# A decoder layer on one core: the input's norm ahead of the memory's, and the memory's projections spread over the attention

## The reference

```python
h = rmsnorm(x, norm1_g); z = h @ w_in      # pool 512 | q 1024 | k 128 | v 128 | memory q 512 | gates 3072
y_pool = pool_mixer(u_pool)                # 4 groups, trailing windows 2, 4, 8, 16, then a 128x128 map
y_swa = sliding_attention(rope(q), rope(k), v, sinks)   # 16 heads of 64, 2 key heads, window 128
km, vm = split(rmsnorm(mem, mem_norm_g) @ w_mem_kv)     # 256 tokens x (512 | 512)
y_mem = softmax(qm @ km.T * 128 ** -0.5) @ vm           # 4 heads of 128
x = x + (g0 * (y_pool @ wp) + g1 * (y_swa @ ws) + g2 * (y_mem @ wm)) @ w_out
x = x + peer(rmsnorm(x, norm2_g))          # 128 x 128 single-neuron experts, product keys
return rmsnorm(x, final_norm_g)
```

## Time and profile before

| | us |
|---|---|
| median of 3 runs (lowest, highest) | 2134.08 (2133.06, 2134.82) |
| the profiled execution | 2133.81 |
| its span, first to last instruction | 2132.0 |
| PE busy in the span | 2071.6 |
| VectorE busy | 1226.4 |
| ScalarE busy | 792.1 |
| GpSimd busy | 849.2 |

### The profile page before, as it was taken

One profiled execution on the slowest core, in us unless ns is written; L12 is line 12 of the kernel. 1 busy time (PEld: TensorE's weight loads), 2 busy tenths in 40 slices (PEclk: granted clock), 3 DMA queues, 4 the chain that ended last, 5 costly groups with the idle time before them and its releaser, 6 DMA issues.

```text
span 2132.0 us, 30302 instructions
## 1 busy us (share of the span) xinstructions
PE 2071.6 (97%) x10616; PEld 1708.8 (80%) x10616; DVE 1226.4 (58%) x1851; ACT 792.1 (37%) x1136; POOL 849.2 (40%) x361
## 2 busy tenths in 40 slices
PE   6988899999999999999999999999999999999998
PEld 5766788887888888888888888888888888888886
DVE  6678321112129999777777777025555555555556
ACT  5566522323223222344554455332222222222223
POOL 4411144443335444433333333444444444444443
PEclk9999999999999999999999999999999999999999
DMA  5211022222224444446556556665555555565552
GB/s 207 89 40 40 30 99 96 92 97 89 78 79 133 148 138 147 143 118 191 189 196 197 188 191 197 212 222 219 179 182 196 217 184 179 183 224 189 184 182 102
DMA packets 108516, 323.47 MB, mean 152 GB/s; under 512 B 11200, under 2 KB 11200, under 8 KB 106304
## 3 DMA queue, kind: packets, MB, share of 16 engines
q1 hardware_dynamic: 108192, 322.49, 44.9%
q10 hardware_dynamic: 288, 0.54, 0.1%
HBM read 253.78 MB, written 69.21 MB: 151 GB/s over the span
## 4 chain that ended last, share of the span: by engine, by line
issue 47%; PE 32%; POOL 19%; DMA 1%; POOLq 0%; DVE 0%; SPq 0%; ACT 0%
PE bank L637 32%; POOL w_lo L417 19%; DMA a_in<-a_rows 0%; POOLq L416 0%; DVE x_sb L1384 0%; DMA a_rows<-abuf 0%; POOLq L420 0%; DVE x_sb L1379 0%; DVE wf L1358 0%; POOL mask L401 0%; POOL mask L403 0%; SPq L266 0%; DVE wT_lo L1362 0%; ACT wT_hi L994 0%; POOL mask L398 0%
## 5 line engine op out<-in xcount | busy, mean ns | idle before, releaser
L417 POOL TENSOR_TENSOR w_lo<-raw,w_hi 128x1024 fp32r<-128x1024 f32 x346 | 845.5, 2444 | 1264.1 <-ACT w_hi L763 1264.1
L763 ACT ACTIVATE w_hi<-raw 128x1024 fp32r<-128x1024 f32 x346 | 366.7, 1060 | 1216.5 <-PE bank L440 698.7
L440 PE MATMUL bank<-hT_hi,w_hi 128*128 128x512 f32 x1488 | 590.9, 397 | 0.5 <-POOL w_lo L417 0.4
L440 PE MATMUL bank<-hT_hi,w_lo 128*128 128x512 f32 x1488 | 580.5, 390 | 0.0
L440 PE MATMUL bank<-hT_lo,w_hi 128*128 128x512 f32 x1488 | 579.3, 389 | 0.0
L1362 DVE TENSOR_TENSOR wT_lo<-wf,wT_hi 128x512 fp32r<-128x512 f32 x128 | 313.5, 2449 | 131.0 <-ACT wT_hi L994 131.0
L440 PEld LDWEIGHTS bank<-hT_hi,w_lo 128*128 128x128 f32 x1488 | 279.4, 188 | 59.9
L440 PEld LDWEIGHTS bank<-hT_hi,w_hi 128*128 128x128 f32 x1488 | 279.8, 188 | 58.7 <-issue 3.9
L440 PEld LDWEIGHTS bank<-hT_lo,w_hi 128*128 128x128 f32 x1488 | 280.1, 188 | 56.1 <-issue 0.7
L637 PE MATMUL bank<-w_hi,wT_hi 128*128 128x512 f32 x1024 | 315.3, 389 | 0.1
L637 PE MATMUL bank<-w_lo,wT_hi 128*128 128x512 f32 x1024 | 315.3, 389 | 0.0
(11 more groups left out here) (217 smaller groups left out, 1518.9 us busy)
## 6 DMA issues: line engine op xcount, KB each, us to landing
raw<-stream SPq DMA_DIRECT2D x346, 512.0 KB, 3.4
a_rows<-abuf SPq DMA_DIRECT2D x128, 256.0 KB, 4.0
g_rows<-gstage SPq DMA_DIRECT2D x32, 1024.0 KB, 6.2
g_in<-g_rows SPq DMA_DIRECT2D x16, 2048.0 KB, 9.3
a_in<-a_rows SPq DMA_DIRECT2D x128, 256.0 KB, 3.5
x_sb<-x SPq DMA_DIRECT2D x4, 512.0 KB, 8.5
out<-x_sb SPq DMA_DIRECT2D x4, 512.0 KB, 2.6
subkeys<-subkeys SPq DMA_DIRECT2D x1, 1024.0 KB, 14.5
```

The lines of the kernel that those rows point to most:

```text
L417: pool.tensor_tensor(w_lo[:, k % 2, :], raw[:, k % RAW, :], w_hi[:, k % 2, :].bitcast(f32), ALU.subtract).then_inc(lo_ready, 1)
L440: last = pe.matmul(dst, w[:, slot, k * P:(k + 1) * P], rhs[low][:, r0 + k - k0, :], start=(k == k0 and wi == 0), stop=(k == k1 - 1 and wi ...
L763: act.activation(w_hi[:, base % 2, :], raw[:, slot, :], ACT.Copy).then_inc(hi_ready, 1)
```

## The change

- The order of the chunks: K, V, the pool groups, two queries, then by turns one chunk of the memory and one query (memory's values first, four, then its keys), then the last two of the memory's queries.
- The loads of x come first, on two queues; x is squared by ScalarE (tiles 0, 2) and VectorE (tiles 1, 3), normed in place and turned at once, all eight k into eight banks. The memory is squared, normed and turned later: its transposes stand behind the second pool group, its halves behind the third pool window. x is loaded again for the residual behind chunk 31.
- Angles and sines are computed after the low halves of x instead of before.
- The pool groups' projections are read by ScalarE (`pool_input`), where VectorE had copied and negated them.
- In the attention, `window_values(u-1)` takes the memory's chunk u (`memory_filler`) in its turn n = 1, behind the transposes and ahead of the first product with V. Its bank is 0. ScalarE reads it (`filler_out`) between the second and the third copy of probabilities, and does one more `split` in each turn, between `outputs_high` and the exponentials. Value chunks are now computed transposed, with 24 matmuls of 256 columns, and turned one pair later with two transposes.
- GpSimd does its subtraction in four pieces of 256 columns for chunks 0 to 23.

```diff
...
-S_KM, S_VM, S_K, S_V, S_POOL = 0, 4, 8, 9, 10
-S_Q, S_QM, S_GATE = 14, 22, 26
+S_K, S_V, S_POOL, S_GATE = 0, 1, 2, 26
+S_Q = (6, 7, 9, 11, 13, 15, 17, 19, 21, 23, 24, 25)
+S_MEM = (8, 10, 12, 14, 16, 18, 20, 22)
...
+            load_x(0)
+            load_x(2)
             for n in range(2):
                 load(n, n, fresh=True)
-            for t in range(TT):
-                sp.dma_start(x_sb[:, t, :], dram["x"][t * P:(t + 1) * P, :]).then_inc(x_loaded[t], 16)
+            sp.dma_start(freq[:, :], dram["freq"]).then_inc(pos_loaded, 16)
+            sp.dma_start(pos_i[:, :], dram["positions"].broadcast_to([P, T])).then_inc(pos_loaded, 16)
+            for t in range(MT):
+                sp.dma_start(mem_sb[:, t, :], dram["mem"][t * P:(t + 1) * P, :]).then_inc(mem_loaded, 16)
...
+            with sp.Fori(RAW, S_GATE + 6 - RAW + 1, RAW) as n0:
+                for k in range(RAW):
+                    load(n0 + k, k)
+            sp.wait_ge(chunk_used, S_MEM[-1] + 1)
+            for t in range(TT):
+                load_x(t)
...
+            def low(n, k, pieces=1):
                 pool.wait_ge(hi_ready, n + 1)
-                pool.tensor_tensor(w_lo[:, k % 2, :], raw[:, k % RAW, :], w_hi[:, k % 2, :].bitcast(f32),
-                                   ALU.subtract).then_inc(lo_ready, 1)
-            with pool.Fori(0, CHUNKS // RAW * RAW - RAW + 1, RAW) as n0:
+                for at in range(0, D, D // pieces):
+                    cols = slice(at, at + D // pieces)
+                    last = pool.tensor_tensor(w_lo[:, k % 2, cols], raw[:, k % RAW, cols],
+                                              w_hi[:, k % 2, cols].bitcast(f32), ALU.subtract)
+                last.then_inc(lo_ready, 1)
+            with pool.Fori(0, QUARTERED - RAW + 1, RAW) as n0:
+                for k in range(RAW):
+                    low(n0 + k, k, pieces=4)
...
             pe.wait_ge(consts, 1)
+            for t in range(TT):
+                pe.wait_ge(normed, t + 1)
+                for k in range(KC):
                     last = pe.transpose(bank[k][:, t * P:(t + 1) * P],
-                                        memn[:, t, k * P:(k + 1) * P], ident[:, :])
-                last.then_inc(turned, 1)
-            for h in range(4):
-                project(S_KM + h, R_KM + h, memT, cols=M, before=split_ready(0) if h == 0 else None)
-                if h >= 1:
-                    turn(xn, MT + 1, KC, h - 1, first=True)
-            for q in range(4):
-                chunk(S_VM + q)
-                for k in range(2):
-                    for m in range(MT):
-                        for low_m, w in ((0, w_hi), (0, w_lo), (1, w_hi)):
-                            last = pe.matmul(bank[2 + m][:, :], memT[low_m][:, 2 * q + k, m * P:(m + 1) * P],
-                                             w[:, q % 2, k * T:(k + 1) * T],
-                                             start=(q == 0 and k == 0 and low_m == 0 and w is w_hi),
-                                             stop=(q == 3 and k == 1 and low_m == 1))
-                last.then_inc(chunk_used, 1)
-                turn(xn, MT + 1, KC, 3 + q, first=True)
-            turn(xn, MT + 1, KC, KC - 1, first=True)
-            project(S_K, R_K, hT, before=split_ready(KC))
-            project(S_V, R_V, hT)
+                                        x_sb[:, t, k * P:(k + 1) * P], ident[:, :])
+                    if t == TT - 1:
+                        last.then_inc(turned, 1)
+            project(S_K, hT, 0, 0, before=split_ready(0))
+            project(S_V, hT, 1, 0)
...
+            def turn_mem():
+                pe.wait_ge(normed, TT + MT)
+                for k in range(KC):
+                    for t in range(MT):
+                        at = k % 2 * M + t * P
+                        last = pe.transpose(bank[2 + k // 2][:, at:at + P],
+                                            mem_sb[:, t, k * P:(k + 1) * P], ident[:, :])
+                    last.then_inc(turned, 1)
...
+                n = S_POOL + gi
+                project(n, hT, n % 2, n - 1)
...
+                if gi == 1:
+                    turn_mem()
...
+            def memory_filler(u):
+                n = S_MEM[u]
+                turns = 1 <= u <= 4
+                project(n, memT, 0, n, cols=M, used=not turns)
+                if turns:
+                    for m in range(MT):
+                        last = pe.transpose(bank[0][:, M + m * P:M + (m + 1) * P], vmT[:, m * P:(m + 1) * P],
+                                            ident[:, :])
+                    last.then_inc(chunk_used, 1)
+            def window_values(u, filler=None):
...
+                    if n == 1 and filler is not None:
+                        memory_filler(filler)
...
-                    window_values(u - 1)
-                project(S_Q + u + 2, R_Q + u + 2, hT, strict=(u > 0))
+                    window_values(u - 1, filler=u)
+                else:
+                    memory_filler(0)
+                project(S_Q[u + 2], hT, 0, S_Q[u + 2])
...
+            def pool_input(gi):
+                n = S_POOL + gi
+                act.wait_ge(chunk_used, n + 1)
+                act.wait_ge(proj_read, n)
+                if gi >= 1:
+                    act.wait_ge(mixed, gi)
+                act.activation(ub[:, PAD:], bank[n % 2][:, :], ACT.Copy).then_inc(proj_read, 1)
+            def mem_high(k):
+                act.wait_ge(turned, KC + k // 2 * 2 + 2)
+                act.activation(memT_hi[:, k, :], bank[2 + k // 2][:, k % 2 * M:(k % 2 + 1) * M], ACT.Copy,
+                               scale=gains[:, 1, k:k + 1]).then_inc(turned_hi, 1)
...
+                pool_input(gi)
                 split(S_POOL + gi + 2)
                 if gi == 0:
                     double_keys()
                 if gi == 1:
                     place_values()
-                if gi >= 1:
+                    mix_high(0)
+                if gi == 2:
+                    for k in range(KC):
+                        mem_high(k)
+                if gi >= 2:
                     mix_high(gi - 1)
...
+            def filler_out(u):
+                act.wait_ge(chunk_used, S_MEM[u] + 1)
+                if 1 <= u <= 4:
+                    act.activation(vm[:, :, (u - 1) * P:u * P],
+                                   bank[0][:, M:2 * M].rearrange("p (m c) -> p m c", m=MT), ACT.Copy)
+                if u < 4:
+                    act.activation(vmT[:, :], bank[0][:, 0:M], ACT.Copy).then_inc(proj_read, 1)
+                else:
+                    act.activation(kmT[:, u - 4, :], bank[0][:, 0:M], ACT.Copy).then_inc(proj_read, 1)
...
+                split(S_Q[u + 1] + 2)
                 next_q(u)
                 if u >= 1:
-                    turn_probs(TT, 4 * (u - 1))
+                    turn_probs(TT, 4 * (u - 1), which=(0, 1))
+                filler_out(u)
+                if u >= 1:
+                    turn_probs(TT, 4 * (u - 1), which=(2, 3))
                     outputs_high(8 + u - 1, u)
+                split(S_MEM[u] + 2)
...
+                turned_q = (2 + u, S_Q[u + 1] % 2 if u == 0 else 0, qr[:, (u + 1) % 2, :])
+                if u == 0:
+                    rotate_bank(*turned_q)
...
+                if 0 < u < 7:
                     rotate_bank(*turned_q)
...
+    memory = [cols(w_kv, slice((4 + h) * P, (5 + h) * P)) for h in range(4)]
+    memory += [cols(w_kv, slice(h * P, (h + 1) * P)) for h in range(4)]
+    chunks = [cols(w_in, slice(k0, k0 + P)), cols(w_in, slice(v0, v0 + P))]
     chunks += [cols(w_in, slice(gi * P, (gi + 1) * P)) for gi in range(4)]
-    chunks += [cols(w_in, slice(q0 + c * P, q0 + (c + 1) * P)) for c in Q_ORDER]
-    chunks += [cols(w_in, slice(m0 + h * P, m0 + (h + 1) * P)) for h in range(4)]
+    chunks += queries[:2]
+    for u in range(8):
+        chunks += [memory[u], queries[u + 2]]
+    chunks += queries[10:]
...
```

More of the change, by code:

```diff
@@ L448, in _, with project, turn @@
             yT = (yT_hi, yT_lo)
-            def project(n, rn, rhs, cols=T, strict=False, before=None):
+            def project(n, rhs, b, read, cols=T, before=None, used=True):
                 chunk(n)
[L453 to L462, removed]
+                if read:
+                    pe.wait_ge(proj_read, read)
+                product(bank[b][:, 0:cols], n % 2, rhs, before=before, used=used)
+            def turn(src, tok_ready, base, k):
+                pe.wait_ge(turned_lo, base + max(k - 3, 0))
                 for t in range(TT):
@@ L767, in _, with root @@
             step(act.activation(std[:, 7:8], eps[:, :], ACT.Sqrt))
[L768 to L774 removed]
+            def root(col, cols=1):
+                act.activation(std[:, col:col + cols], ssum[:, col:col + cols], ACT.Sqrt, scale=1.0 / D,
+                               bias=eps[:, :]).then_inc(std_ready, 1)
+            for t in range(TT):
+                if t % 2 == 0:
+                    act.wait_ge(x_loaded[t], 16)
```

(34 more changed lines are left out.)

218 lines of the change are left out of this document (89 added, 129 removed).

## The result

| | before | after |
|---|---|---|
| median of 4 runs each (lowest, highest), us | 2134.03 (2133.06, 2134.82) | 2148.91 (2147.57, 2152.41) |
| the profiled execution and its span, us | 2133.81, 2132.0 | 2150.03, 2148.0 |

The ratio is 1.0073, 95% interval 1.0058 to 1.0088: the change makes the kernel 0.7% slower. I had forecast 2152.

A forecast was written before the change was run, and what follows sets the result against it. PE, busy 97% of the span, bounds the kernel; the attention is a ring of VectorE and ScalarE. 2133.8 - 31.4 (front) + 36.5 (turns) + 13.5 (clock) = 2152.4, forecast 2152 us, range 2122 to 2166.

The forecast's parts named there:

- K ends, first mix, scores 0: Front: K's projections end near 19 us, PE's first mix starts at 40.5, pair 0's first scores at 68.5.
- pair 0 ready for its exponentials: End of the front: pair 0's masks and maxima done at 78.8 us, where it was 110.18.
- the front: All ahead of the attention's exponentials: reordering gives back 31.4 us, bounds 26 and 38.
- turns 1 to 6, clock included: Attention, one pair a turn: 20.6 us for turns 1 to 4, 20.25 for 5 and 6, plus 2.2 of clock each.
- of it the clock: Attention: PE partly at half clock behind its gap, 2.2 us in each of six turns, 13.5 lost; bounds 0 and 5.2.
- turn 7: Last of the seven attention turns: bank 0 is read early, chunk starts near 0.3 us before the masks, turn 16.8 us.
- the second read of x: Load between chunks 31 and 32: hidden under the gates' projections, 0 us; without that cover, 5 us.
- chunk 0 costs nothing there: Front: the memory's chunk 0 runs behind scores 0 while VectorE has 5 us of masks and maxima; 0 us.
- The ring through PE: Attention: from the masks' start t, bank 0's wait, chunk, values, output copy, split and exponentials run in series; 36.5 us lost.
- some 10 us higher: Attention: by the skill's clock section, the clock term is near its upper bound and the total some 10 us higher.
- GpSimd in fourths, 0: Attention's scaling: pieces hold VectorE the same 2.1 us in sum, so 0; bounds 2.1 a turn won, about 0.3 lost.

The follow-up runs named there:

- e6: The changed kernel with 11 unused matmuls in PE's wait ahead of the memory's chunk in turns 1 to 6: 2138.35 us, ratio 1.0023.
- e1: The changed kernel with VectorE reading q(u+1) out of bank 0 ahead of pair u's masks in every turn: 2128.74 us, ratio 0.9979.
- e3: The changed kernel with the memory's chunk behind the values instead of ahead of them, still in bank 0: 2121.81 us, ratio 0.994.
- e8: The kernel before with only GpSimd's subtraction in four pieces for chunks 0 to 23: 2121.62 us, ratio 0.9944.
- e2: The changed kernel with 32 unused matmuls ahead of the memory's chunk in turns 1 to 6: 2191.19 us, ratio 1.027.
- e5: The changed kernel with the memory's chunk in bank 1 behind the query's projection, its read counted by its own semaphore: 2111.01 us, ratio 0.9897.
- e7: The changed kernel with all eight memory chunks in one block behind scores 0, banks 0 and 1 by turns: 2128.67 us, ratio 0.9983.
- e10: e5 with ScalarE's split for the next query chunk moved behind the next turn's swap: 2109.03 us, ratio 0.9886 against the kernel before.
- e9: The kernel before, GpSimd whole, with ScalarE's split behind the swap instead of ahead in the first eight turns: 2124.37 us, ratio 0.9961.

## Why the prediction came out right, step by step

| step | predicted | measured |
|---|---|---|
| K ends, first mix, scores 0 | 19, 40.5, 68.5 | 20.2, 40.7, 69.0 |
| pair 0 ready for its exponentials | 78.8 | 79.15 |
| the front, by pair 0's `den` | -31.4 | -28.3 |
| turns 1 to 6, clock included | 22.8, 22.45 | mean 22.0 |
| of it the clock | 2.2 | 2.0 (e6) |
| turn 7 | 16.8 | 14.8 |
| the second read of x | 0 | at most 0.5 |

- **The front.** Right up to the maxima. The step that failed is "chunk 0 costs nothing there", and most of it is the clock, for which the sum had no term in this place. PE had stood for 2.94 us, the chunk took 5.5 us instead of 2.94, and with its reader, `split` and the table load behind it on ScalarE the exponentials came 2.9 us after the maxima. At full clock (e6) the same four end 0.3 us before the maxima. What is left there is 0.9 us: the pieces of GpSimd that follow this `split` lie beside two small steps of VectorE behind the maxima (`mcap`, `negm`), which take 0.53 and 0.67 us instead of 0.17 each. The other 2.1 were not simply to be had. Where the clock was full at chunk 0 it had been half at the first mix, and pair 0's `den` stayed where it was. From e6's 86.38 - 71.19 = 15.19 us between first scores and `den`, and first scores at 69.00, I estimate 84.2 for a front with neither.
- **The ring through PE.** Right, piece by piece: the wait ends by `rotate_bank` at t + 3.07 (I had t + 3.1), the values take 3.48 (3.5), the exponentials follow `split` and not the maxima. e1 shortens this wait and e3 covers it, and they get back 20 and 27 us, the clock's share included, so it is shown and not only read. At full clock (e6) a turn took 20.04 us where the ring's terms gave 20.6 and 20.25. The scaling and what stands with it took 4.4 instead of 4.7, which is most of the difference.
- **The clock.** The size was near (2.2 against 2.0), and e6 separates it from the ring. That was in part luck: 2.2 was a choice between 0 and 5.2. (Six times 2.2 is 13.2, not the 13.5 of the sum.) The Trainium skill, "TensorE: Matmul & The Clock Gate", section on HAM oscillation, describes such a new fall and warm-up in each round. The trace agrees: the granted clock is 0.92 or 0.85 in turns 1 to 6 and 1.00 in turn 7. But the sum that I had set beside it, some 10 us higher, did not come: the chunk takes 4.3 or 5.3 us, and the values behind it run at full clock already (98.54 to 102.02, 3.48 us).
- **Turn 7.** Mis-sized by 2.0: bank 0 was free early, as I had read. The chunk started at 221.00, 1.9 us before the masks (222.93) and not 0.3 before them, at full clock, and the turn took 14.8 us, as long as most in the kernel before.
- **GpSimd in fourths, 0.** Wrong as a step, though inside its bounds. In the kernel after the pieces save 3.6 (span) to 6.3 us (median), nearly all in the front. In the turns they save next to nothing (0.6 us in seven), as forecast: the scaling takes 4.07 there against 4.28. In the kernel before they save 12 (e8). My bounds came from the right rows, but I asked how long an instruction is and not what stands beside it. The rule can be looked up: the Trainium skill, "SBUF — State Buffer", section "Who interferes with whom", says that a VectorE instruction in its two-port mode or with two inputs in SBUF shares a port pair with GpSimd and that whichever comes second stands until the other ends, while one outside that mode with at most one input in SBUF doesn't contend. The traces agree: scaling 4.28 beside GpSimd and 2.19 without, masks (scores in PSUM, mask in SBUF) 2.47 and 2.48 either way.
- The errors partly cancel, and that is luck: +3.1 in the front, -2.0 in turn 7, -4.2 in the other six (the ring, the clock and the 0.3 of the sum). Their total, -3.1, takes 2152.4 to 2149.3; the profiled execution took 2150.0, and what follows pair 7 makes up 0.5 of the rest.

Left open: in e2, e5, e6, e7 and e10 the first scores come at 71.1 to 71.3 and in e3 at 72.2, in the kernel after and in e1 at 69.0 and 68.8. In the later ones PE starts K 0.4 to 0.9 later (its transposes of x took 5.9 to 6.4 instead of 5.3 us), and the first mix, behind a wait of 3.0 us as in the others (2.96 and 3.06), took 2.07 or 2.08 instead of 1.13. e2 and e6 have the same program up to there as the kernel after, so the edit alone isn't the reason. Why the clock fell at the first mix in some and at chunk 0 in others no run here shows. With one trace for each kernel, a difference of 2 us in the first scores says nothing about an edit.

## What to carry to other kernels

Work that fills an engine's idle time must not stand ahead of the work that others wait for: PE had room for 2.94 us in each turn. Ahead of the values and behind a late bank seven chunks cost the turns 43.8 us. In a free bank behind everything else (e5) the turns lost 2.9, and what follows them another 2.9. For every wait in the inner loop ask what is queued behind it, in the lists of its readers too. When two engines slow each other down, move one of the instructions beside something it doesn't disturb before making it smaller.

## What was not expected of the hardware

- A filler of work for nobody made the kernel 10.6 us faster (e6).
- The length of the gap alone doesn't tell the clock behind it. Ahead of chunk 0 PE stood for 2.90 us in e1 and in e6: the chunk then took 5.45 us at a granted clock of 0.50 (1.2 GHz) in e1 and 2.95 at 1.00 (2.4 GHz) in e6. In e1 itself it took 5.3 us behind 2.49 us in turn 1 and 2.94 behind 2.47 in turn 2.
- Place and not length of GpSimd's instruction: one move of ScalarE's `split`, no work saved, is worth 8.3 us of the kernel before (e9, by its ratio).
- An f32 matmul of 128 rows by 256 columns took 0.43 us, the fp32r ones of the chunk 0.12, both from starts at full clock.
